# One layer of a gated and sparse-attention block: output steps, late selection steps and norms in another order, and a third transposition bank for attention tiles 0 to 3

## Time and profile before

| | us |
|---|---|
| median of 3 runs | 565.14 (564.82 to 565.28) |
| the profiled execution | 565.3 |
| its span, first to last instruction | 563.5 |
| PE busy | 545.6 (97%) |
| VectorE busy | 444.0 (79%) |
| ScalarE busy | 371.5 (66%) |
| GpSimd busy | 180.0 (32%) |

### The profile page before, as it was taken

How to read it: one execution, slowest core, us unless ns; L and a number is a source line. 1 busy time by engine, 2 the same in 40 slices (tenths; PEclk the granted TensorE clock), 3 DMA queues, 4 the chain that set the end, 5 groups by cost and what they waited for, 6 DMA issues and landing times. The chain is left out here.

```text
span 563.5 us, 8936 instructions
## 1 busy us (share of the span) xinstructions
PE 545.6 (97%) x2974; PEld 461.4 (82%) x2974; DVE 444.0 (79%) x1107; ACT 371.5 (66%) x711; POOL 180.0 (32%) x283
## 2 busy tenths in 40 slices
PE   8999999999999999999999999989999999999997
PEld 8997788878888888887888887768788789889886
DVE  4775777899889998999878888887878787866631
ACT  5885667767997767777988566756465555755510
POOL 1760000014449997667210003551112021202130
PEclk9999999999999999999999999999999999999999
DMA  8623110012331111131212144503030302011032
GB/s 250 214 66 110 57 38 20 1 38 76 112 93 39 38 46 49 39 94 39 56 58 74 52 133 134 170 19 95 19 94 20 94 19 76 20 40 35 1 113 75
DMA packets 39982, 39.69 MB, mean 70 GB/s; under 512 B 6144, under 2 KB 28160, under 8 KB 39936
## 3 DMA queue, kind: packets, MB, share of 16 engines
q1 hardware_dynamic: 38416, 39.11, 22.9%
q10 hardware_dynamic: 1520, 0.01, 0.1%
HBM read 30.72 MB, written 8.39 MB: 69 GB/s over the span
## 5 line engine op out<-in xcount | busy, mean ns | idle before, releaser
L1072 PE MATMUL ps_proj<-w_hi,xT_hi 128*128 128x512 f32 (+1 forms) x432 | 164.7, 381 | 1.2 <-DVE w_lo L1382 1.0
L1072 PE MATMUL ps_proj<-w_lo,xT_hi 128*128 128x512 f32 (+1 forms) x432 | 161.1, 373 | 0.0
L1072 PE MATMUL ps_proj<-w_hi,xT_lo 128*128 128x512 f32 (+1 forms) x432 | 161.1, 373 | 0.0
L912 ACT ACTIVATE ps_lg<-score,cand 128x768 f32<-128x768 f32 (+2 forms) x96 | 96.0, 1000 | 10.4 <-DVE cand L1475 10.4
L1072 PEld LDWEIGHTS ps_proj<-w_lo,xT_hi 128*128 128x128 f32 x432 | 81.4, 188 | 14.8
L1072 PEld LDWEIGHTS ps_proj<-w_hi,xT_hi 128*128 128x128 f32 x432 | 81.4, 189 | 14.5 <-DVE w_lo L1382 2.0
L1072 PEld LDWEIGHTS ps_proj<-w_hi,xT_lo 128*128 128x128 f32 x432 | 81.5, 189 | 11.8
L969 ACT CAST xT_hi<-ps_tp 128x512 fp32r<-128x512 f32 (+3 forms) x96 | 43.0, 483 | 66.0 <-PE ps_tp L1193 66.0
L1696 DVE TENSOR_TENSOR xT_lo<-ps_tp,xT_hi 128x512 fp32r<-128x512 f32 (+3 forms) x96 | 50.4, 553 | 31.4 <-ACT xT_hi L969 31.1
L1382 DVE SCALAR_TENSOR_TENSOR w_lo<-stage,g_in,w_hi 128x512 fp32r<-128x512 f32 x48 | 43.1, 905 | 10.0 <-ACT w_hi L772 9.2
L953 ACT ACTIVATE lo_f<-lo_f,negmax 128x128 f32<-128x128 f32 (+7 forms) x64 | 50.2, 785 | 0.2
(11 more groups left out here) (175 smaller groups left out, 1101.7 us busy)
## 6 DMA issues: line engine op xcount, KB each, us to landing
stage<-in_w_in_dram SPq DMA_DIRECT2D x48, 256.0 KB, 2.7
x_in<-in_x_dram SPq DMA_DIRECT2D x8, 512.0 KB, 6.0
lo_f<-in_x_dram SPq DMA_DIRECT2D x7, 512.0 KB, 4.0
out_dram<-lo_f SPq DMA_DIRECT2D x7, 512.0 KB, 3.5
q_scratch<-nat SPq DMA_DIRECT2D x8, 256.0 KB, 2.1
q_in<-q_scratch SPq DMA_DIRECT2D x8, 256.0 KB, 3.6
stage<-in_w_out_dram SPq DMA_DIRECT2D x8, 256.0 KB, 2.7
z_scratch<-nat SPq DMA_DIRECT2D x8, 256.0 KB, 2.1
```

Source lines behind the costliest of these rows:

```text
L912: act.activation(ps_lg[i % 2][:, 0:keys(t)], score[:, sc_off[t]:sc_off[t] + keys(t)], ACT.Sign, bias=cand[:, t:t + 1].bitcast(F32), scale= ...
L1072: mm = pe.matmul(ps_proj[u % 2][:, 0:n], a[:, k, rows], b[:, k, 0:n], start=(k == 0 and i == 0), stop=(k == KB - 1 and i == 2))
```

## The change

It has eight parts. Line numbers of the changed kernel are 10 to 26 higher; pT is L1213, the exponential L964, hi_pT L980, lo_pT L1722, bias_max L1712, hi_mix L1008, w_hi L782, w_lo L1402, lo_q L1613, the scan L1551, y_sums L1740, add_res L1758, counts L1485.

1. IQ's weights are split one tile behind KVI instead of two. The keys of tile 6 are normalised after the last of them, and transposed at k == 2 of the first IQ unit.
2. `qiT(t+1)` stands behind block 1 instead of 2, for t > 2.
3. q_norm(0) and the first background step move behind the sum of heads of tile 7.
4. A third transposition bank: the upper half of `ps_lg[0]`, for every key of the plan from ("q", 0) to ("p", 3, 4, 0). The ring is three long there. Before the scores of head m = 32 TensorE waits till the third bank's last user has been read.
5. `STEPS` is a table by head instead of 2 everywhere: h=1 and 3 do three steps, 7 and 0 one. The sum by tile stays 16.
6. `W_AT`: each block of O2's weights one head earlier, but for the fourth, which stays at head 17.
7. `add_res(t-2, 0)` from h == 4, behind lo_q, to h == 3.
8. `LATE_AT`: t=1 gives up its step at h=6, and tiles from 4 on take their late steps at odd heads.

```diff
-    IQ_W_BEHIND = 2
+    IQ_W_BEHIND = 1
...
+        ps_tp.append(ps_lg[0][:, BANK:2 * BANK])
...
-        tp_slot = {key: n % 2 for n, key in enumerate(tp_plan)}
+        tp_wide = range(tp_plan.index(("q", 0)), tp_plan.index(("p", 3, 4, 0)) + 1)
+        tp_slot = {}
+        for n, key in enumerate(tp_plan):
+            if n == 0 or n == tp_wide.stop:
+                turn = itertools.cycle(range(2))
+            elif n == tp_wide.start:
+                turn = itertools.cycle((n % 2, 1 - n % 2, 2))
+            tp_slot[key] = next(turn)
+        third_users = [key for key in tp_plan if tp_slot[key] == 2]
...
-        W_AT = (16, 16, 17, 17, 20, 21, 22, 23)
+        W_AT = (15, 15, 16, 17, 19, 20, 21, 22)
...
-                if t > 0:
+                if 0 < t < T - 1:
                     hi_k(t - 1)
...
+            hi_k(T - 2)
...
             def tp(key):
 
                 assert tp_plan[len(issued)] == key
-                if len(issued) >= 2:
-                    pe.wait_ge(*tp_release(issued[-2]))
+                slot = tp_slot[key]
+                if slot in slot_user:
+                    pe.wait_ge(*tp_release(slot_user[slot]))
                 issued.append(key)
-                return ps_tp[tp_slot[key]]
+                slot_user[slot] = key
+                return ps_tp[slot]
...
-                    if k == 2 and t + 1 < T:
+                    if k == (2 if t <= T0 else 1) and t + 1 < T:
                         qiT(t + 1)
...
-                if t > 0:
+                if 0 < t < T - 1:
                     kT(t - 1)
+
+            def late_keys(k):
+                if k == 2:
+                    kT(T - 2)
+
             for t in range(T0, T):
                 if t == T0:
-                    project(IQ, t)
+                    project(IQ, t, late_keys)
...
+                if m == 4 * H:
+                    pe.wait_ge(*tp_release(third_users[-1]))
                 dot_keys(ps_lg[m % 2], q_stack[t % 2], h, k_hh, k_ll, keys(t)).then_inc(s_done, 1)
...
-            STEPS = 2
+            STEPS = {1: 3, 2: 2, 3: 3, 4: 2, 5: 2, 6: 2, 7: 1, 0: 1}
...
-                    steps = STEPS_BZ[m] if m < len(STEPS_BZ) else STEPS
+                    steps = STEPS_BZ[m] if m < len(STEPS_BZ) else STEPS[h]
...
-                if t > 0:
+                if 0 < t < T - 1:
                     lo_k(t - 1)
...
+            lo_k(T - 2)
...
+                if t == 1:
+                    background(True, False)
+                    q_norm(0)
                 if t >= 2:
                     lo_w(KB * AV + t)
                 q_sums(t)
+                if t == 0:
+                    continue
                 background(True, False)
                 q_norm(t)
...
-            LATE_AT = ((2, 4, 6), (2, 4, 6), (0, 2, 4, 6))
+            LATE_AT = ((2, 4, 6), (2, 4), (0, 2, 4, 6), (0, 2, 4, 6), (1, 3, 5, 7))
...
+                    if h == 3 and t > 1:
+                        add_res(t - 2, 0)
                     if h == Q_AT and t + 1 < T:
                         lo_q(t + 1)
-                    if h == 4 and t > 1:
-                        add_res(t - 2, 0)
...
-                    if h in LATE_AT[min(t, 2)]:
+                    if h in LATE_AT[min(t, 4)]:
                         next(late, None)
```

More of the change, by code:

```diff
@@ L30 @@
+import itertools
 from contextlib import ExitStack
@@ L1033, in _ @@
         def _(pe):
-            issued = []
+            issued, slot_user = [], {}
             def tp(key):
                 assert tp_plan[len(issued)] == key
-                if len(issued) >= 2:
-                    pe.wait_ge(*tp_release(issued[-2]))
+                slot = tp_slot[key]
+                if slot in slot_user:
+                    pe.wait_ge(*tp_release(slot_user[slot]))
                 issued.append(key)
-                return ps_tp[tp_slot[key]]
+                slot_user[slot] = key
+                return ps_tp[slot]
             def xT(t):
@@ L1274, in _ @@
             scores(0, 1)
-            STEPS = 2
-            assert STEPS * H == 2 * KB
+            STEPS = {1: 3, 2: 2, 3: 3, 4: 2, 5: 2, 6: 2, 7: 1, 0: 1}
+            assert sum(STEPS.values()) == 2 * KB
             pending = last_projections()
@@ L1299, in _ @@
                         scores(*divmod(m + 2, H))
-            for _ in range(STEPS):
+            for _ in range(STEPS[0]):
                 next(pending)
```

## The result

The changed kernel takes 573.48 us (median of 5 runs, 573.32 to 574.16); the kernel before, in the same runs, 565.2. The ratio is 1.0149, with a 95% interval of 1.0135 to 1.0163. It is slower by 8.3 us, where 2.0 us less was forecast; the range ended at 566.8. The profiled execution has a span of 572.4 us.

The account below looks back on a forecast made before the run. TensorE, busy 97% at clock 1.00, was taken as the bound, so only its pauses could change. 565.3 - 3.7 (projections) - 2.5 (tiles 0 to 3) + 4.2 (tiles 4 to 7) = 563.3 us; 8-in-10 range 559.5 to 566.8.

Parts of the forecast that it names:

- (e): Attention, tiles 2 and 3: the residual add ahead of lo_q leaves 0.4 of TensorE's wait; -0.85 us in each.
- (h): One output step instead of two: +0.27 for h=7 of tiles 2 and 3, +0.3 at the head after tile 3.
- (j): Tiles 4 and 5, h=3: a late step right ahead of lo_q costs +1.0 in tile 4, +1.65 in tile 5.
- (k): Tiles 4 and 5, h=7: a late step ahead of add and mix, +0.9 and +0.55; tile 7's start +0.3.
- (a, b, c): Projections: khat wait goes and w_lo's shrinks, -1.1; four relu_sb waits go, -1.2; the 1.22 one goes, -1.38.
- (d): Start of tile 2: third bank removes bank waits, but the first output step waits for the mix; 1.5 uncashed, +0.9 lost.
- (f): Output weights one head earlier: TensorE's 1.65 wait for w_lo goes, -1.81, with +0.3 back for VectorE's order.
- (g): Attention, tiles 0 to 3: pT(24)'s bank wait goes, -0.57; a scan taken off h=4, -0.2.
- (i): Tile 4: the scan in front of turn_y goes, -1.35; small ones at other even heads, -0.6.
- (j, k, l): Tiles 4 to 7: (j), (k), and less cover for h=7 exponentials, +0.95 over tiles 4 to 6, +0.8 in tile 7.
- Rival B: Late steps behind odd heads fall into VectorE's idle time, so (j) and (k)'s 4.1 cost nothing: 559.2 us; chance 0.17.
- Rival D: Every late step at an odd head from tile 4 delays transposed probabilities, 7.5 exposed: 566.7 us; chance 0.12.

Follow-up runs that it names:

- two steps: Changed kernel with two output steps per head everywhere and the add back behind lo_q at head 4: 565.41 us.
- part 8 alone: The kernel before with only part 8 (late steps) put in: 570.64 us.
- short scans: Changed kernel with the scans of tiles 4 to 7 going over 64 keys instead of all: 565.85 us.
- scan at head 1: Author's version (parts 1 to 3, third bank, two steps, only O2's last weight block early), tile 5's 1024-key scan moved from head 0 to 1: 557.69 us.
- parts 5 and 7 alone: The kernel before with only the table of output steps and the add at head 3 put in: 575.86 us.
- two banks: Kernel before with parts 1 to 3, O2's last four weight blocks one head early, add ahead of lo_q in tiles 2 and 3, two banks: 561.30 us.
- part 8 undone: Changed kernel with LATE_AT as before and all else changed: 565.73 us.
- odd heads only: Changed kernel with half of part 8 undone: t=1 keeps its late step at head 6, odd heads from tile 4 stay: 570.31 us.
- scan at head 3: Author's version (parts 1 to 3, third bank, two steps, only O2's last weight block early), tile 5's 1024-key scan at head 3, ahead of lo_q: 560.78 us.

## Why the prediction was wrong

Two steps failed. What stands ahead of the add in tile 2 and of the mix after tile 3 was not worked out ((e), and with it (h)): there the scans hold TensorE. And the clock, taken as 1.00 throughout, was put at nothing. (j) and (k) had the right places and were 2.3 too small.

- (a, b, c) Right. The khat wait is gone and a loss of 0.40 (43.11 to 43.74, less 0.23) is left of the w_lo wait; four of the five relu waits are gone, the 1.22 among them, and one of 0.38 stays. Of the 0.9 beyond the forecast 0.2 isn't the change's: before waits 0.39 for x at 8.65, this run doesn't. The rest lies in small losses that I had not summed.
- (d) Right: the first output step waits 1.90 for the mix. From head 15 to head 17 the changed kernel loses 1.6, but 0.7 of that is the third step that now stands at head 17; with two steps it is 1.0, where 0.9 was forecast. ScalarE's row: 1.33 for the two weight blocks at 349.86, ahead of both casts of the mix.
- (e) Failed, and first. "In front ... 0.4 stays: -0.85" took the add alone and not what the shifted late steps put in front of it: the scan, 360.24 to 363.03. The wait grew from 1.08 to 1.84, where 0.4 was to be left. The prediction says that the late steps come later because t=1 gives one up, and works out no place of it in tiles 2 and 3. The same omission hid the 1.79 at 406.15, where the kernel before doesn't wait. These two waits are 3.6 in all; less the 0.4 and the 0.3 that (e) and (h) left there, some 3 of the 4.3 missed in tiles 0 to 3.
- (f) Half right: 0.39 of the w_lo wait is left, of 1.65. But it isn't a gain beside part 5; it pays for it.
- (g) Right: pT of head 24 doesn't wait. (h) Right for the exponentials; for the head after tile 3 it had 0.3, and the 896 scan made it the 1.79 above.
- (i) Right: turn_y in tile 5 doesn't wait.
- (j, k, l) Right in every place but the start of tile 7, where no pause came (0.3 forecast). In losses lo_q costs 1.22 and 2.44 (1.0 and 1.65 forecast), the mix 1.45 and 1.42 (0.9 and 0.55), each last head 0.2 to 0.3 and head 63 1.34. That VectorE's idle time and earlier pauses would give some back was wrong; that is the 2.3 missed in tiles 4 to 7. Rival B, that these steps are covered, is refuted by part 8 alone. Rival D was nearest in mechanism, and too low, since its steps are only those from tile 4.
- The clock. "Each pause costs some 0.16 more than its idle time" was read from a kernel whose longest pause in attention is 1.65 and whose clock was 1.00. Three pauses of 1.8 to 2.3 were each followed by a stretch at half clock, 1.7 each and 5.1 in all at most. The prediction put this term at nothing; it wasn't among the rivals, and beside the scans it is the largest term of the miss. The Trainium skill ("TensorE: Matmul & The Clock Gate", HAM oscillation) says that waits between bursts of matmuls put the clock down again, and that the price is half of the time spent there. The trace agrees on the price: 3.4 us at 0.5, 1.7 at most, three times. The page tells it of waits of 3 to 5 us; here the falls came with pauses of 1.8 to 2.3, and the pause of 1.90 at 353.04 had none.

What stays open: that the pauses bring the clock down rests on the runs in which they are absent (short scans; scan at head 1 against head 3), not on a row that names the cause; why the pause of 1.90 at 353.04 (and those of 1.93 and 2.29 with two steps) leaves the clock alone and that of 1.79 at 406.15 doesn't; why the same kernel falls in some runs only; and how much of the 5.1 would be waits without it.

## What to carry to other kernels

When a list of leftover work is drawn on by position, taking one entry out moves every later one; follow each long item (here the scans of 1.75 to 2.29 us) to its new place, and ask what stands right behind it. Two edits that look like separate gains may be one edit and its price (steps per head and the heads of the weights), so measure a part alone before it is given a sign. A pause of TensorE of about 2 us should be priced with the clock that may follow it, here up to 1.7 us.

## What the runs showed of the hardware

- The low stretches ahead of the last matmul are all 3.4 us long, two behind one another in the kernel with parts 5 and 7 alone (380.3 to 387.1). They start 0.1 to 1.5 us after TensorE resumes, but for one with part 8 alone, which starts at 458.8, 0.2 before the end of the pause at 459.03. Half of 3.4 in 570 is 0.003 of mean clock, so the means of single runs count them: by that the kernel before has one in 5 of 25 runs. What the runs with one take more differs: 0.1 to 0.2 with two banks, 1.0 in before, 1.6 with short scans, 2.3 with part 8 undone. Waits behind a stretch can hide part of it; why the last is more than 1.7 isn't shown, since no such run was profiled.
- The scan of 768 keys took 1.75 in before and 2.79 here. It starts at 360.24 while GpSimd is in an instruction with two inputs:

```profile
360.12 1.30 POOL L720 TENSOR_TENSOR lo_f<-hi_f,lo_f 128x512 f32<-128x512 f32 x1
```

In the version with two steps the scan starts first (359.63, 1.75 long) and that instruction takes 2.71. The one that comes second waits for the other: the scan reads eq twice, GpSimd's has 1.18 us to go when it starts, and it takes 1.04 longer. By that some 1.0 of the 1.84 that TensorE waits at 363.86 comes from this meeting (an estimate). The Trainium skill ("SBUF — State Buffer", Who interferes with whom) says that a VectorE instruction with two SBUF inputs and a GpSimd one that reads SBUF exclude one another, and that the one issued first goes through; the trace agrees.
- Four kernels (part 8 undone, parts 5 and 7, odd heads only, scan at head 3) end 4.7 to 4.8 us after the start of their last matmul, all others 3.5 to 3.6. In the last 8 us exactly these four have the row

```profile
q14 instruction: 1, 0.01, 0.2%
...
out_dram<-res_last SPq DMA_DIRECT2D x2, 256.0 KB, 2.6
```

where the others have no instruction packet and 2.0 us to landing (2.6 is the middle of 2.0 and 3.2, the last store's). Why it falls there in these four isn't shown; 1.2 us of each of their totals goes with it, so the table's "end" is the fairer comparison.
